# Side products beside the ranking, bias step functions over all queries, state-space scalars in the feed-forward

## The reference, cut to what matters

```python
h = rms_norm(x, attn_norm[l]); proj = h @ w_in[l]          # 6,984 columns: aq ak av iq ik iw bq bf bi bg cq ckv ckpe gates
# A: which keys a query may see, and its bias
score = einsum(relu(iq . ik), iw) * idx_scale              # per query block of 128, causal
_, sel = lax.top_k(score, 128)
bias = rel_bias[t5_bucket(pb[:, :, None] - p_sel)]         # 32 buckets by distance, 4 heads
# B: recurrence with decay exp(b_t - b_s), b a running sum of log f, heads of 128
attn = einsum('bhtk,bhsk,bhtsk->bhts', qc, kc, decay); o = inter + attn @ v
# gates, feed-forward
mixed = g_a * (o_a @ w_up_a) + g_b * (o_b @ w_up_b) + g_c * (o_c @ w_up_c); x = x + mixed @ w_out
x = x + (silu(h @ w_gate) * (h @ w_up)) @ w_down
# second block, state space: scalars of each state that depend on inputs alone
dt = exp(log_dt); lam_bar = exp(lam * dt); b_bar = ((lam_bar - 1.0) / lam)[..., None] * b
```

## Time and profile before

| | |
|---|---|
| median of three runs | 1759.74 us |
| profiled execution, its own time | 1759.97 us |
| its span | 1758.2 us |
| PE busy | 1499.6 us, 85% |
| PE weight loads busy | 1131.0 us, 64% |
| DVE busy | 994.2 us, 57% |
| ACT busy | 465.1 us, 26% |
| granted TensorE clock, mean | 0.911 |

### The profile page before, as it was taken

How to read it: one execution, slowest core, us unless ns; L and a number is a source line. 1 busy time by engine, 2 the same in 40 slices (tenths; PEclk the granted TensorE clock), 3 DMA queues, 4 the chain that set the end, 5 groups by cost and what they waited for, 6 DMA issues and landing times.

```text
span 1758.2 us, 19877 instructions
## 1 busy us (share of the span) xinstructions
PE 1499.6 (85%) x7694; PEld 1131.0 (64%) x7694; DVE 994.2 (57%) x1696; ACT 465.1 (26%) x740; POOL 16.3 (1%) x11
## 2 busy tenths in 40 slices
PE   4993788896899788799799999979768999859988
PEld 2852778784576555588488888868427954446753
DVE  6249755655365767775545545443493652867841
ACT  2345232331232001422323333422223121114410
POOL 0000000000000000000000000000000000200000
PEclk8996889898999667899899999989889999979989
DMA  4211011122222111153133444112302211600001
GB/s 185 85 44 52 25 49 48 48 103 69 96 85 77 32 37 37 49 193 145 45 120 146 168 171 158 55 66 99 118 25 60 72 55 65 240 24 1 1 1 48
DMA packets 39740, 140.56 MB, mean 80 GB/s; under 512 B 13024, under 2 KB 17376, under 8 KB 27104
## 3 DMA queue, kind: packets, MB, share of 16 engines
q1 hardware_dynamic: 34464, 130.52, 20.8%
q10 hardware_dynamic: 5184, 8.78, 1.4%
HBM read 128.41 MB, written 8.39 MB: 78 GB/s over the span
## 4 chain that ended last, share of the span: by engine, by line
PE 49%; DVE 7%; ACT 1%; issue 1%; SPq 1%; DMA 0%; ACTq 0%; DVEq 0%; POOL 0%; POOLq 0%
PE turn L667 20%; PE score L652 8%; PE score L667 4%; PE sum L652 3%; PE turn L652 3%; PE sum L667 2%; PE sum L1165 2%; PE score L1139 1%; PE score L1070 1%; PE turn L1151 1%; DVE work L1564 1%; SPq L593 1%; DVE work L1633 0%; PE turn L1043 0%; PE turn L770 0%
## 5 line engine op out<-in xcount | busy, mean ns | idle before, releaser
L1633 DVE TENSOR_TENSOR ring_r<-ring,heads_r 128x1024 fp32r<-128x1024 f32 (+3 forms) x153 | 176.3, 1153 | 215.8 <-ACT heads_r L1234 179.9
L1234 ACT ACTIVATE heads_r<-ring 128x1024 fp32r<-128x1024 f32 (+3 forms) x153 | 153.4, 1002 | 278.4 <-DMA ring<-wstream 130.3
L667 PE MATMUL score<-h_sb_r,heads_r 128*128 128x512 f32 x368 | 152.1, 413 | 0.0
L667 PE MATMUL turn<-tiles_r,heads_r 128*128 128x512 f32 x336 | 133.6, 398 | 0.0
L667 PE MATMUL turn<-h_sb_r,heads_r 128*128 128x512 f32 x304 | 119.6, 393 | 8.1 <-DVE ring_r L1633 8.1
L667 PE MATMUL score<-x_sb_r,heads_r 128*128 128x512 f32 x248 | 110.8, 447 | 13.1 <-DVE h_sb_r L1633 13.1
L667 PE MATMUL turn<-wide_r,heads_r 128*128 128x512 f32 x312 | 121.6, 390 | 0.0
L667 PE MATMUL turn<-wide_r,ring_r 128*128 128x512 f32 x312 | 121.6, 390 | 0.0
L667 PE MATMUL score<-x_sb_r,ring_r 128*128 128x512 f32 x248 | 104.3, 421 | 0.0
L652 PE MATMUL score<-h_sb,ring 128*128 128x512 f32 x160 | 72.9, 614 | 16.3 <-ACT h_sb L1441 16.3
L667 PEld LDWEIGHTS score<-h_sb_r,heads_r 128*128 128x128 f32 x368 | 75.1, 204 | 14.1 <-issue 0.2
(11 more groups left out here) (386 smaller groups left out, 2983.3 us busy)
## 6 DMA issues: line engine op xcount, KB each, us to landing
ring<-wstream SPq DMA_DIRECT2D x95, 1024.0 KB, 4.9
ring<-wstream SPq DMA_DIRECT2D x16, 704.0 KB, 4.2
ring<-gated SPq DMA_DIRECT2D x6, 1024.0 KB, 7.0
gated<-tiles ACTq DMA_DIRECT2D x17, 256.0 KB, 2.3
x_sb<-xT SPq DMA_DIRECT2D x4, 512.0 KB, 5.7
x_sb<-xT ACTq DMA_DIRECT2D x1, 2048.0 KB, 8.1
outT<-x_sb SPq DMA_DIRECT2D x1, 2048.0 KB, 6.3
gated<-probs ACTq DMA_DIRECT2D x7, 256.0 KB, 2.4
```

Source lines behind the costliest of these rows:

```text
L667: return pe.matmul(out, a, w, **k) if moving else pe.matmul(out, w, a, **k)
L1234: step(act.activation(head_piece(p), chunk(name)[:, c:c + cols], ACT.Identity), f"head {p}")
L1633: step(dve.tensor_tensor(out, a, b, op), name)
```

## The change

Four edits:

1. `PLACES` has eight new places `rank 0` to `rank 7` with two steps each. The recurrence has one step in every place (32 steps; it was 44), the bias has twelve places with six steps (it was 10 steps). The total stays 86. PE calls the new places right after the last projection of bq; ACT after its preparation of the recurrence; DVE makes the rests at four points of the ranking of block 2 and in the first head's preparation.
2. The multiplication of the output gate bg moves from the third head to the second.
3. Bias: one part for each key block, over all its query blocks (4, 3, 2 and 1). A step matrix has up to 512 columns; there are four buffers of 512 columns, and the products go to four banks, S, U and O. A semaphore `bias_done` frees the banks, and attention A starts after the last part has been added.
4. The state-space scalars are made in the feed-forward (tiles 7 to 11), by the same instructions.

```diff
-PLACES = [(f"rec {h} {l}", 1 + (l in (2, 5, 7))) for h in range(4) for l in range(LEVELS + 1)] + [(f"tail {i}", 2) for i in range(4)] + \
-         [("latent 0", 2), ("latent 1", 4)] + [(f"mla {i}", 1) for i in range(18)] + [(f"bias {i}", i % 2) for i in range(20)]
+PLACES = [(f"rank {i}", 2) for i in range(8)] + [(f"rec {h} {l}", 1) for h in range(4) for l in range(LEVELS + 1)] + \
+         [(f"tail {i}", 2) for i in range(4)] + [("latent 0", 2), ("latent 1", 4)] + [(f"mla {i}", 1) for i in range(18)] + \
+         [(f"bias {i}", 1 - i % 2) for i in range(12)]
...
     def STEPS(g, cols):
-        return part(work, 2 * T + g % 8 * 2 * P, cols)
+        return part(work, (2 + g % 4) * T, cols)
...
-    BIAS_PARTS = [(0, (0, 1)), (0, (2, 3)), (1, (1, 2)), (1, (3,)), (2, (2, 3)), (3, (3,))]
+    BIAS_PARTS = [(0, (0, 1, 2, 3), (S[0], S[1], U[0], U[1])), (1, (1, 2, 3), (O[0], S[0], S[1])),
+                  (2, (2, 3), (U[0], U[1])), (3, (3,), (O[0],))]
+    BIAS_FREE = [0, 2, 4, 5]
...
@@ tensor
+            for i in range(8):
+                beside(f"rank {i}")
             V = ROW[:, :, 200:712]
             for h in range(4):
...
-            for c_, (key, queries) in enumerate(BIAS_PARTS):
-                banks = [turn_bank()]
-                if len(queries) == 2:
-                    n_ = tally.count["turn_full"] + 1
-                    pe.wait_ge(turn_done, n_ - 1)
-                    banks.append(U[n_ % 2])
+            pe.wait_ge(turn_done, tally.count["turn_full"])
+            pe.wait_ge(score_done, tally.count["score_full"])
+            pe.wait_ge(sum_done, sums[0])
+            for c_, (key, queries, banks) in enumerate(BIAS_PARTS):
+                if c_:
+                    pe.wait_ge(bias_done, BIAS_FREE[c_])
                 for g in range(32):
                     pe.wait_ge(dve_step, at(f"steps {c_} {g}"))
                     for e, b in enumerate(banks):
                         for z in range(3):
                             mm = pe.matmul(b[:, 16 * g:16 * g + 16], STEPS_B(g, e), REL[z],
                                            start=(z == 0), stop=(z == 2))
...
-                    if (32 * c_ + g) % 9 == 8 and (32 * c_ + g) // 9 < 20:
-                        beside(f"bias {(32 * c_ + g) // 9}")
+                    mm.then_inc(steps_used if g < 31 else bias_full, 1)
+                    up(steps_used if g < 31 else bias_full, f"bias {c_} {g}")
+                    if g % 12 == 7:
+                        beside(f"bias {3 * c_ + g // 12}")
+            pe.wait_ge(bias_done, 10)
@@ scalar
+            for i in range(8):
+                beside(f"rank {i}")
             for h in range(4):
...
                 weight_heads(2)
                 if 2 <= j < 6:
                     head(f"hidden {j - 2}", HIDDEN_HEAD[j - 2], TL[:, j - 2, :])
+                if j == 7:
+                    step(act.activation(SC["dt"], sm("log_dt"), ACT.Exp), "dt")
+                if j == 10:
+                    act.wait_ge(dve_step, at("ssm turn"))
...
             weight_heads(8)
-            step(act.activation(SC["dt"], sm("log_dt"), ACT.Exp), "dt")
-            act.wait_ge(dve_step, at("ssm turn"))
...
             weight_heads(20)
@@ vector
+                if i in (11, 13):
+                    beside(f"rank {i // 2 - 2}")
             choose(2)
+            beside("rank 5")
+            beside("rank 6")
...
                 tt(e4, b4[:, :, P - 1:P].broadcast_to([P, 4, P]), b4, ALU.subtract, f"rec args {h}")
+                if h == 0:
+                    beside("rank 7")
                 dve.wait_ge(act_step, at(f"rec el {h}"))
...
-                    if h == 2 and l < 4:
+                    if h == 1 and l < 4:
                         dve.wait_ge(gemm_done, at(f"tanh bg {l}"))
...
                 for g in range(32):
-                    if g >= 8:
-                        dve.wait_ge(steps_used, at(f"bias {c_} {g - 8}"))
+                    if g >= 4:
+                        dve.wait_ge(steps_used, at(f"bias {c_} {g - 4}"))
...
+                dve.wait_ge(bias_full, c_ + 1)
+                for n, b in zip(queries, banks):
                     lo = upto(n) + key * P
...
+                if j == 8:
+                    ssm_turns()
+                if j == 11:
+                    ssm_scalars()
...
             def squares_final(j):
-                if j == 0:
-                    ssm_scalars()
                 if j < 6:
                     squares("final", j, SQUARES[j])
```

## The result

| | before | after |
|---|---|---|
| median | 1759.67 us (4 runs, 1758.51 to 1760.82) | 1703.62 us (4 runs, 1700.04 to 1707.66) |
| ratio after / before | | 0.9682, 95% interval 0.9660 to 0.9705 |
| profiled execution, span | 1758.2 us | 1701.6 us |
| PE / DVE / ACT busy | 85 / 57 / 26% | 88 / 58 / 27% |
| mean granted clock | 0.911 | 0.922 |

The account below looks back on a forecast made before the run. With PE busy 85% of the span, time was taken to go where PE waits or its clock is low. 1759.97 - 19.1 - 24 - 13.2 = 1703.7 us; own range 1697 to 1711, all cases but the slower one 1691 to 1722.

Parts of the forecast that it names:

- Ranking and recurrence: Sixteen side steps added in the ranking, twelve removed from the recurrence: +14.5 and -33.6 us, together -19 us.
- +14.5: Ranking: the first head's cross products end at 206.5 instead of 192.0 us, behind the sixteen added steps.
- a row step (24 products of 256 columns) is taken as the same: Recurrence: a removed row step saves the same 2.8 us as other side steps, because the columns are the same.
- the waits between heads ... keep their steps: 0: Waits between the recurrence's heads, and all stages from the tail to the MLA, contribute 0 us.
- bound of -22: Ranking and recurrence: -22 us instead of -19 if the clock stays up in the second pause.
- the second pause: Ranking: PE waits 7.6 us before the ninth side step, until 179.6 us; 2.4 us added for half clock afterwards.
- The slower rival: Recurrence loses its clock because PE could idle between levels with one step a place: +94 us, 1797 us; chance 3%.
- Bias: Bias stage falls from 112.4 to 88 us, -24 us, with four fewer side steps the larger part.
- the price of 0.0637 us for a product at half clock: Bias: 54 products took 3.44 us back to back at clock 0.50, so PE bounds the first two parts at half clock.
- 5.3 us each: Bias: the time a side step takes at half clock, counted in the sum by PE.
- Scalars: Moving the state-space scalars removes the down projection's hole and the slow clock behind it: -13.2 us.
- The hole: Down projection, 1145.6 to 1156.4 us: PE does nothing for 10.80 us while DVE makes scalars before needed rests.

Follow-up runs that it names:

- experiment 1: Changed kernel with the four 128-column row steps behind the aq and ak half tiles, or ahead of the 256-column steps: 1693.52 and 1692.75 us.
- six_products: Changed kernel with each group of three bias products issued twice, 1920 products instead of 960: 1714.34 us.
- experiments 7 and 4: 7: changed kernel, narrow steps later, rests earlier, six bias side steps in latent attention, 1690.57 us; 4: kernel before, new bias stage, ten side steps kept, 1740.64 us.
- s_alone: Kernel before with only the state-space scalars moved into the feed-forward: 1750.73 us, ratio 0.9954.
- no_scalars: Changed kernel with the state-space scalars back in the down projection: 1720.70 us, ratio 0.9782.
- experiment 5: State-space scalars alone moved into the feed-forward of the kernel before, at two positions (1750.73, 1752.03 us), or put back in the changed kernel (1720.70 us).
- cq1_first: Changed kernel with the four 128-column row steps ahead of the 256-column ones, ending the first head: 1692.75 us, ratio 0.9621.
- cq1_late: Changed kernel with the four 128-column row steps behind the ten half tiles of aq and ak: 1693.52 us, ratio 0.9632.

## Why the prediction came out right, and where its steps were wrong

- **Ranking and recurrence, -19 forecast, -10.1 measured.** The steps in the ranking held: resumption at 156 and 178.8 (forecast 157 and 179.6), last side step 203.0 (203.8), cross products 206.1 (206.5). The first head ended 5.7 us later; +14.5 less three steps of 2.8 us is 6.1. The third and fourth heads gave 7.5 and 9.5 us for 8.4. The step that failed is "a row step (24 products of 256 columns) is taken as the same", with "the waits between heads ... keep their steps: 0". The change sets the four row steps of 128 columns behind the wait of the second head. There the clock, though PE was nearly full, stayed at half for 34 us, and the head took 53.1 us instead of 52.0 less 8.4. With them elsewhere (experiment 1) the recurrence ended at 360.8 and 358.9, 22 and 24 us earlier than before. The forecast's bound of -22 had another cause, a clock that stays up in the second pause.
- **The slower rival** (the recurrence loses its clock) had the right danger by the wrong cause. It looked for PE gaps at each level, and there are none of weight. The clock fell in the wait between two heads, as it does in every head, and in one of them it did not come back for 34 us.
- **Bias, -24 forecast, -31.7 measured.** The failed step is the price of 0.0637 us for a product at half clock, from the earlier trace rows. That row joins 54 products because their modelled ends overlap the next starts; its 3.44 us are nine groups of 0.38, DVE's own pace for 256 columns (0.353 and a gap). The price was DVE's, read from PE's row, and the products of the earlier trace rows were not back to back, as the forecast called them; those of `six_products` were. The earlier trace rows held the hint: 19.3 of PE's 26.0 us of idle time were ended by DVE. With the true price PE is the bound in a side step alone, no stretch at full clock is needed, and the stage costs DVE's 54 us, the additions and some 3 us a side step. The Trainium skill, "TensorE: Matmul & The Clock Gate", section "Wait — 56ns, not 53.3ns?", says that starts of products, however narrow, never come closer than some 25 ns. This case's trace agrees (0.025 us at full, 0.027 at half clock). A floor does not rule out 0.064, but it would have been a reason to look again.
- **Side steps in the bias.** I took 5.3 us each as PE's. They are 4.0 to 5.0 us long but cost 2.9 to 3.0 (experiments 7 and 4); DVE makes up to four matrices ahead meanwhile.
- **Scalars, -13.2 forecast, -13.6 alone, -16.2 in the changed kernel.** The hole is gone as forecast: 121.6 us without a gap from 1070.7 on, with the feed-forward not slower. What lies beyond is in part the half clock that begins in the 24 products of one column at the end of the feed-forward (L987): 6.8 us before and in `s_alone`, 3.4 in after, 10.2 in `no_scalars`, with the same code there. The products of 512 columns behind them start every 0.43 us at half clock and every 0.23 at full, so that about half of such a stretch is lost (an estimate): 1.7 of the 2.6 us between 13.6 and 16.2, and all of the 3.4 between 13.6 and the 17.0 of experiment 5. The remaining 0.9 us is open.
- **The sum** was right by luck: +8.9 in the recurrence and -7.7 in the bias met, with +1.5 in the attentions and -3.0 behind them. The range of 1691 to 1722 was wide enough for each alone. Whether the spread of after's own runs, 1700 to 1708, is the second head's clock, its one profile cannot tell.

## What to carry to other kernels

Look which products come first behind a wait of PE. Behind waits of the same 4.65 us between heads the clock was at half for 3.4 to 10.2 us, mostly 6.8, where they had 256 or 512 columns, and for 13.7 or 34 where they had 128; reordering independent work was worth 10 us here. Take the price of an operation from a stretch where its engine waits for nothing, never from a row in which another engine feeds it. Before a difference of some microseconds is put down to an edit, compare stretches in which both kernels run the same instructions: here they differed by up to 6.6 us.

## What the runs showed of the hardware

- The granted clock stayed at 0.50 for 34 us with PE 95% busy on products of 128 columns, and returned once a step of 512 columns stood there. In two other kernels, `six_products` and `no_scalars`, it came back within the same narrow steps, after 13.7 us. Where products of 256 or 512 columns stood first it was at half for 6.8 us in `cq1_first` and `cq1_late`, and 3.4 to 10.2 over all kernels; in the second head before, where it was 10.2, one more wait of 1.5 us lay in it. It did not fall in products of 128 columns that began at full clock.
- The clock also fell where PE had no gap. It fell in products of 16 columns in `six_products` (at 568.6 us, 2.9 us after the first of them, and stayed at half for the 12.3 us that PE went on with them), in those of 24 columns in block 2, and in those of one column at the end of the feed-forward (at 1070.8 us in after, after 5.3 us of them).
- The Trainium skill, "TensorE: Matmul & The Clock Gate", section "What's actually happening", has the clock set by how busy PE has been recently. The heads with wide products first agree (6.8 us at half); the 34 us at 95% busy and the falls without a gap do not, if busy is taken as the share of time in which the profile shows an instruction on PE.
- A product of 128 columns started every 0.214 us at half and 0.112 at full clock; of 16 columns every 0.027 and 0.025.
- The same block 2 took 509.4 or 516.0 us. The clock was at half for 3.4 and 6.8 us longer in two of its stretches, and came back 3.4 us later in a third.
